# Ordering the columns of the network projections' matmuls in interleaved runs, on one Trainium2 core

## The reference

```python
def _swiglu(x, w_gate, w_up, w_down):
    return (jax.nn.silu(x @ w_gate) * (x @ w_up)) @ w_down

# first block: network 1, token mixers, memory cross attention, network 2
h = _layer_norm(ALPHA * h + 0.5 * _swiglu(h, ffn1_w_gate[l], ffn1_w_up[l], ffn1_w_down[l]), ln1_g[l], ln1_b[l])
...
h = _layer_norm(ALPHA * h + 0.5 * _swiglu(h, ffn2_w_gate[l], ffn2_w_up[l], ffn2_w_down[l]), ln4_g[l], ln4_b[l])
# second block: attention and pooling, then network 3
x = x + (jax.nn.silu(h @ w_gate[l]) * (h @ w_up[l])) @ w_down[l]
```

## Time and profile before

| | us |
|---|---|
| median of the 2 runs shown | 1665.95 (1665.79 and 1666.12) |
| span of the profiled execution, first to last instruction | 1663.7 |
| TensorE busy in it | 1653.9 (99%) |
| TensorE weight loads (beside the matmuls) | 1393.3 (84%) |
| POOL, DVE, ACT busy | 704.5, 629.7, 597.6 |
| mean granted TensorE clock | 0.999 of 2.4 GHz |

### The profile page before, as it was taken

One profiled execution on the slowest core, in us unless ns is written; L12 is line 12 of the kernel. 1 busy time (PEld: TensorE's weight loads), 2 busy tenths in 40 slices (PEclk: granted clock), 3 DMA queues, 4 the chain that ended last, 5 costly groups with the idle time before them and its releaser, 6 DMA issues.

```text
span 1663.7 us, 20763 instructions
## 1 busy us (share of the span) xinstructions
PE 1653.9 (99%) x8375; PEld 1393.3 (84%) x8375; DVE 629.7 (38%) x1059; ACT 597.6 (36%) x911; POOL 704.5 (42%) x392
## 2 busy tenths in 40 slices
PE   9999999999999999999999999999999999999999
PEld 7888888899888888889888888898768988888888
DVE  4111121257565777656121111257763512121122
ACT  4122222247545555436221222247574322122220
POOL 4454444554572443133454444444323444344442
PEclk9999999999999999999999999999999999999999
DMA  7333243333222444123333243351113333323332
GB/s 208 91 102 92 83 117 89 101 104 111 77 64 64 127 129 144 57 77 89 91 99 101 74 117 99 92 156 42 44 32 80 86 101 93 97 83 110 99 89 77
DMA packets 296041, 157.58 MB, mean 95 GB/s; under 512 B 5265, under 2 KB 292618, under 8 KB 295946
## 3 DMA queue, kind: packets, MB, share of 16 engines
q1 hardware_dynamic: 295946, 156.26, 32.8%
HBM read 154.14 MB, written 2.10 MB: 94 GB/s over the span
## 4 chain that ended last, share of the span: by engine, by line
PE 93%; DVE 3%; ACT 2%; issue 1%; DMA 1%; POOL 0%; SPq 0%; DVEq 0%; POOLq 0%
PE bank L551 22%; PE bank L552 22%; PE bank L555 22%; PE bank L2349 2%; PE bank L2353 2%; PE bank L2350 2%; PE bank L594 2%; PE bank L595 2%; PE bank L599 2%; PE bank L2846 2%; PE bank L574 1%; PE bank L580 1%; PE bank L575 1%; PE bank L2834 1%; PE bank L2375 1%; PE bank L2594 1%
## 5 line engine op out<-in xcount | busy, mean ns | idle before, releaser
L479 POOL TENSOR_TENSOR wlo<-wraw,whi 128x1024 fp32r<-128x1024 f32 (+1 forms) x238 | 561.4, 2372 | 771.3 <-ACT whi L474 771.3
L551 PE MATMUL bank<-ahi,whi 128*128 128x512 f32 x1294 | 507.8, 392 | 0.0
L552 PE MATMUL bank<-alo,whi 128*128 128x512 f32 x1294 | 503.8, 389 | 0.0
L474 ACT CAST whi<-wraw 128x1024 fp32r<-128x1024 f32 (+1 forms) x268 | 268.0, 1025 | 232.6 <-PE bank L555 152.9
L555 PE MATMUL bank<-ahi,wlo 128*128 128x512 f32 x1294 | 320.9, 389 | 0.0
L551 PEld LDWEIGHTS bank<-ahi,whi 128*128 128x128 f32 x1294 | 243.0, 188 | 51.4 <-issue 1.2
L552 PEld LDWEIGHTS bank<-alo,whi 128*128 128x128 f32 x1294 | 242.9, 188 | 51.2 <-issue 1.4
L555 PEld LDWEIGHTS bank<-ahi,wlo 128*128 128x128 f32 x1294 | 242.9, 188 | 50.4
L1649 DVE SCALAR_TENSOR_TENSOR hval<-gate,bank 128x512 f32<-128x512 f32 x66 | 45.4, 687 | 554.4 <-PE bank L555 540.2
L1044 ACT ACTIVATE gate<-bank 128x512 f32<-128x512 f32 x66 | 39.5, 598 | 512.8 <-PE bank L555 500.6
L1658 DVE SCALAR_TENSOR_TENSOR res<-res,bank 128x512 f32<-128x512 f32 x78 | 52.7, 685 | 236.3 <-PE bank L555 163.8
(11 more groups left out here) (380 smaller groups left out, 2285.0 us busy)
## 6 DMA issues: line engine op xcount, KB each, us to landing
wraw<-in_ffn_w_gate SPq DMA_DIRECT2D x42, 512.0 KB, 3.9
wraw<-in_ffn_w_up SPq DMA_DIRECT2D x42, 512.0 KB, 3.9
wraw<-in_ffn_w_down SPq DMA_DIRECT2D x32, 512.0 KB, 3.6
wraw<-in_w_in SPq DMA_DIRECT2D x30, 512.0 KB, 4.0
wraw<-in_w_gate SPq DMA_DIRECT2D x21, 512.0 KB, 3.9
wraw<-in_w_up SPq DMA_DIRECT2D x21, 512.0 KB, 3.9
wraw<-in_w_out SPq DMA_DIRECT2D x16, 512.0 KB, 5.2
wraw<-in_w_down SPq DMA_DIRECT2D x16, 512.0 KB, 3.7
```

What stands on the lines that cost most here:

```text
L474: eng.copy(high_of(b)[:, 0:n], raw_of(b)[:, 0:n]).then_inc(hi_ready, 1)
L479: eng.tensor_tensor(low_of(b)[:, 0:n], raw_of(b)[:, 0:n], high_of(b)[:, 0:n], ALU.subtract).then_inc(LO[b][0], 1)
L551: eng.matmul(o, w, xhi[:, k, :], start=(k == 0), stop=False)
L552: eng.matmul(o, w, xlo[:, k, :], start=False, stop=False)
```

## The change

It gives each part of each network an order in which the 512 columns are visited. An entry (parts, run) means: cut the 512 columns into `parts` equal parts and take `run` columns of the first, `run` of the second, and so on in turn; (2, 16) visits columns 0 to 15, 256 to 271, 16 to 31, 272 to 287 and so on. One column is 4 bytes. `READ_ORDER` applies to the moving operand (`ahi`, `alo`, `hhi`, `hlo`), `WRITE_ORDER` to the bank. Where both have the same entry, each token stays at its place in the bank. The middle part of each network is different: its projection up reads in an order and writes straight on, so that its hidden values stand in that order; its projection down reads them straight on and writes the bank in that order, which puts the tokens back.

```diff
+        READ_ORDER = {"f1_up0": (2, 16), "f1_down0": (2, 16), "f1_up1": (2, 16), "f1_up2": (2, 4), "f1_down2": (2, 4),
+                      "f2_up0": (2, 64), "f2_down0": (2, 64), "f2_up1": (2, 4), "f2_up2": (2, 128), "f2_down2": (2, 128),
+                      "f3_up0": (4, 16), "f3_down0": (4, 16), "f3_up1": (2, 64), "f3_up2": (8, 8), "f3_down2": (8, 8)}
+        WRITE_ORDER = dict(READ_ORDER)
+        for name in ("f1", "f2", "f3"):
+            WRITE_ORDER[f"{name}_down1"] = READ_ORDER[f"{name}_up1"]
+            WRITE_ORDER.pop(f"{name}_up1")
+
+        def ordered(x, orders, ph):
+
+            if ph.name not in orders:
+                return x
+            parts, run = orders[ph.name]
+            return x.rearrange("p (a g e) -> p g a e", a=parts, e=run)
...
         def multiply(eng, ph, j, xhi, xlo, width=T):
 
             b = ph.base + j
-            o = bank_of(ph, j)[:, 0:width]
+            o = ordered(bank_of(ph, j)[:, 0:width], WRITE_ORDER, ph)
             wait_hi(eng, b)
             wait_bank(eng, ph, j)
             for k in range(ph.K):
                 w = high_of(b)[:, k * P:(k + 1) * P]
-                eng.matmul(o, w, xhi[:, k, :], start=(k == 0), stop=False)
-                eng.matmul(o, w, xlo[:, k, :], start=False, stop=False)
+                eng.matmul(o, w, ordered(xhi[:, k, :], READ_ORDER, ph), start=(k == 0), stop=False)
+                eng.matmul(o, w, ordered(xlo[:, k, :], READ_ORDER, ph), start=False, stop=False)
             eng.wait_ge(*LO[b])
             for k in range(ph.K):
-                mm = eng.matmul(o, low_of(b)[:, k * P:(k + 1) * P], xhi[:, k, :],
+                mm = eng.matmul(o, low_of(b)[:, k * P:(k + 1) * P], ordered(xhi[:, k, :], READ_ORDER, ph),
                                 start=False, stop=(k == ph.K - 1))
...
             def multiply_tokens(ph):
                 b = ph.base + LAST
-                at = b % 4, b % RAW
+                at = HI_AT[b] % 4, RAW_AT[b] % RAW
```

More of the change, by code:

```diff
@@ L592, in multiply_hidden @@
                 for j in range(2):
-                    b, o = ph.base + j, bank_of(ph, j)[:, :]
-                    eng.matmul(o, high_of(b)[:, k * P:(k + 1) * P], hhi[:, k, :], start=(k == 0), stop=False)
-                    eng.matmul(o, low_of(b)[:, k * P:(k + 1) * P], hhi[:, k, :], start=False, stop=False)
+                    b, o = ph.base + j, ordered(bank_of(ph, j)[:, :], WRITE_ORDER, ph)
+                    eng.matmul(o, high_of(b)[:, k * P:(k + 1) * P], ordered(hhi[:, k, :], READ_ORDER, ph), start=(k == 0), stop=False)
+                    eng.matmul(o, low_of(b)[:, k * P:(k + 1) * P], ordered(hhi[:, k, :], READ_ORDER, ph), start=False, stop=False)
                 eng.wait_ge(hidden_ready, t0 + k + 1)
                 for j in range(2):
-                    b, o = ph.base + j, bank_of(ph, j)[:, :]
-                    mm = eng.matmul(o, high_of(b)[:, k * P:(k + 1) * P], hlo[:, k, :], start=False, stop=(k == ph.K - 1))
+                    b, o = ph.base + j, ordered(bank_of(ph, j)[:, :], WRITE_ORDER, ph)
+                    mm = eng.matmul(o, high_of(b)[:, k * P:(k + 1) * P], ordered(hlo[:, k, :], READ_ORDER, ph), start=False, stop=(k == ph.K - 1))
                     if k == ph.K - 1:
```

## The result

| | before | after |
|---|---|---|
| median | 1665.95 us | 1702.36 us (1702.17 and 1702.55) |
| span of the profiled execution | 1663.7 us | 1700.4 us |
| ratio of the times | | 1.0223, 95% interval 1.0203 to 1.0242 |

The change makes the kernel 36.4 us slower. The forecast was 1666 with a range of 1624 to 1706: the time lies in the range, the likeliest case did not come.

What follows compares the result with a forecast made beforehand. TensorE bounds the kernel, through the distance between matmul starts. Reads, writes and the last two blocks each counted 0, so 1663.7 us of span + 2.3 around it + 0 = 1666.0 us, range 1624 to 1706.

Steps and rivals of the forecast that it cites:

- the likeliest case: The order leaves the matmul pace at 226.7 ns everywhere: no change, within some 5 us of 1666, chance 0.45.
- What bounds the kernel: TensorE, busy 99% of the span at full clock: time is matmul count times distance between starts, 226.7 ns.
- Writing in runs: 3408 matmuls writing the bank with breaks: 0 taken, bounded by 41.9 us gain and 689 us loss.
- Reading in runs: 3840 matmuls reading moving columns with breaks: 0 per break taken, bounded by 47.2 us gain and 391 us loss.
- the two paces: Matmuls of 256 columns in one run took 117.5 ns each in one stretch and 113.8 in another.
- A price per break: Rival, in the ordered reads: 2.2 ns on each of 177,792 breaks, +391 us (2057); with other worse cases, chance 0.06.
- The rival of short runs: Reads: one extra cycle per fetch of up to 16 columns, runs of 8 and 4 cost more; +37.8 us, 1704, chance 0.17.
- The streams lose their settled state: Rival: interleaved reads keep the uneven 231 ns seen after a start; +4.3 ns on 3840 matmuls, 1682.5 us, chance 0.17.
- The 32 cycles go: Rival: reads lose the 32 cycles beyond one per column, 12.3 ns each, in all or some orders; 1619 to 1650 us, chance 0.15.
- the bound from below: Fastest pace for ordered reads, 214.4 ns a pass of a plain fp32 matmul; 47.2 us on 3840, none taken.
- Two streams that get in each other's way: Weights and moving columns read from SBUF hinder each other by an amount depending on how they stand to each other.

Runs made afterwards that it cites:

- writes alone: The changed kernel with all reads straight on and all its ordered writes kept: 1664.96 us, ratio 0.9998 to the kernel before.
- the smallest weight loads: Blocks of some network parts load only 1 to 96 weight columns in all three products, some parts straight, some in orders: 1695.69 us.
- the shifts: Weight slots moved by 4 to 96 columns, networks 1 and 3 in orders: 1724.8 us; by 1 to 63 columns, everything straight: 1690.01 us.
- the table of orders: The change with twelve other read and write orders, one per part, runs of 2 to 64: 1772.05 us; tabulated with the change's own orders.

## Why the prediction was right and wrong

- *Time and direction.* The range held the time, near its upper end, and the chance for slower by over 2% was 0.23. The likeliest case, no change, was wrong, and the range reached up to the measured time for the sake of a rival whose mechanism is refuted below: that it held is luck.
- *What bounds the kernel.* Right: no instruction moved, the clock stayed, every nanosecond on a matmul reached the end. The ordered stretches are 36.2 us longer, the span 36.8.
- *Writing in runs: 0 taken.* Right, and shown by writes alone. The sentence of the Trainium skill (PSUM — Partial Sum Buffer, Specifications (TRN2)) that any non-contiguous pattern slows matmuls does not hold for these writes, whose runs are 4 columns and more; the milder one that the prediction set beside it (the Trainium skill, Advanced Engine Details and Errata, Memory Cachelines) agrees with them. Its other half, two hits per 16-byte line of SBUF, does not account for the reads: runs of 4, 8 and 16 columns use such lines whole, and they were slower.
- *Reading in runs: "I take 0 per break".* This is the step that failed. It rested on one break in the earlier trace rows standing close to the slower of the two paces in the earlier trace rows. It also leaned on the faster pace coming and going without any change of addresses. The earlier trace rows do not show that, since they compare columns 0 to 255 with columns 256 to 511 and other slots, but it is so: the block at 374.92 above and the one at 352.11 differ in nothing but what ran before them. One break with 128 columns on either side says nothing of 31 or 127 of them: runs of 64 and 128 were free in every run made, as that row suggested, but only 1248 of the 3840 reads were of that kind. The other 2592, with runs of 4, 8 and 16, cost between 4.5 and 24.6 ns each.
- *A price per break.* Also wrong, as assumed: (2,16) has 31 breaks and costs 13.3 ns, (8,16) nearly the same, (4,16) a third, (32,4) with 127 breaks nothing.
- *The rival of short runs.* Its 1704 us was 1.6 us from the measured time, and by accident. It had 0 for (2,16) where 13.3 ns came, and 40 ns for (2,4) where 23.3 came; in us it had 13.1 too little for the runs of 16 and 14.7 too much for those of 4 and 8. Its "one fetch per run of up to 16 columns" would have (2,32) at 226.7 and (32,4) at 266.7 ns; they came at 236.7 and 226.7.
- *The streams lose their settled state.* Half right. It happens, for (8,8) in the three blocks that start afresh (1.8 us of the 36.2), and at 256 ns where 231 was expected. The other orders settle, each at a pace of its own.
- *The 32 cycles go.* Wrong in all 18 orders, at all 19 shifts and with the smallest weight loads: no part's mean was below 226.7 ns, though single distances of 220 ns occur in (32,4). The 214.4 ns taken as the bound from below are half of the 429 ns of a plain fp32 matmul; that it makes two passes is the prediction's reading, and no run shows it. The argument against this rival, that all tiles and slots settle alike at different addresses, was weaker than it looked: in the kernel before, the slots (1152 columns apart), the weight tiles in them (128) and the tiles of activations (512) of the networks' matmuls all stand multiples of 64 columns apart, so none of them differed in the place within 256 bytes, which is what the shifts found to matter.
- *Two streams that get in each other's way.* Borne out by the shifts: 6.6 ns for 64 bytes, and only when the bytes come between the two streams. So the rule of the Trainium skill (SBUF — State Buffer, Who interferes with whom) that TensorE's two read ports are independent and that it waits on nobody is contradicted by this case, for float32r matmuls at this pace. But the same runs show that most of what the change paid for does not move with this meeting: (2,16) is at 240.0 ns at every shift and every load width that was tried, and (2,4), 23.3 ns over 226.7, moved up by 3.3 ns with the shifts and down by 3.3 with a small load.

What stays open: which places of SBUF the moving stream has to visit in turn to lose cycles, that is, the rule behind the table of orders; what the 32 cycles of a straight stream are; why small weight loads make it slower; and how far a pace in the table of orders depends on what ran before it, as it does for (8,8) and for 256 columns. The runs exclude the writes and the absolute address, and they make the size of the weight load unlikely as the main cause; what is left, as an argument and not as a finding, is how the moving stream's own reads follow each other, which was not measured apart from any weight load, since every matmul has one.

## What to carry to other kernels

Where TensorE bounds a kernel with float32r matmuls of 512 columns, read the moving operand straight on or in runs of 64 columns and more; permute on the write side, which was free down to runs of 4 columns. Look at how weights and moving columns stand to each other within 256 bytes: 64 bytes of shift were worth 6.6 ns of 226.7 at 512 columns and 3.5 of 116 at 256, and the best place was not the same for both. When two rows of the same instruction differ in pace, compare what ran before them as well as their addresses. A row with one break bounds one break; before scaling it, or calling it nothing, find a row with many.

## What the runs showed of the hardware that was not expected

- A float32r matmul with 512 moving columns sits at 544 cycles of 2.4 GHz, and several slower means are whole steps of 8 too: 560 (233.3 ns), 576 (240.0), 600 (250.0), 816 (340). Others are not: 231.2, 268.0 and 278.1 ns.
- A weight load of one column takes 0.08 us instead of 0.19, and the matmul beside it gets slower (231.7 ns), not faster.
- In (2,4) neighbouring matmuls alternate between some 254 and some 246 ns and keep doing so for 384 matmuls.
- 64 bytes between activations and weights, with no change of any instruction, made straight projections 2.9% slower (233.3 ns instead of 226.7).
- The same block of 256 columns, with the same code and addresses, runs at 117.9 ns a matmul behind a straight stream and at 113.4 behind one in (2,4).
